# Seven edits to a two-layer trunk: panels asked for before the small vectors, attention's scores group by group, layer 1's first tiles one after the other, and an end that scales its copies

## The reference, cut to what matters

```python
for i in range(DEPTH):
    mod = silu(cond) @ w_ada + b_ada                       # shift, scale, gate, twice
    h = rmsnorm(x, norm_mix) * (1.0 + sc1) + sh1
    mix = mixer_ab(h) if i % 2 == 0 else mixer_c(h)        # layer 0; layer 1
    x = x + g1 * mix
    h = rmsnorm(x, norm_ffn) * (1.0 + sc2) + sh2
    x = x + g2 * ((silu(h @ w_gate) * (h @ w_up)) @ w_down)
return rmsnorm(x, final_norm)
# mixer_ab, attention of a query group: p = softmax(q @ k.T * scale); o = p @ v
# mixer_c, for each of 4 heads: q, k, v, g from h @ w_in; bidirectional scan with
#   decays; y = rmsnorm(y); out += (silu(g) * y) @ w_out
```

## Time and profile before

| | us |
|---|---|
| runs, median (lowest, highest) of 3 | 2038.24 (2036.21, 2041.35) |
| the profiled execution, its own time | 2041.52 |
| its span | 2039.9 |
| PE, weight loads, DVE, ACT busy | 95%, 89%, 58%, 28% |
| mean DMA rate, bytes | 91 GB/s, 185 MB |

### The profile page before, as it was taken

The page is one execution under the profiler, slowest core; times in us unless marked ns, Lnnn a source line. Parts: engine busy times, 40 slices in busy tenths (PEclk is TensorE's granted clock), DMA queues, the critical chain, the costliest instruction groups (busy, mean ns, idle before and its releaser), DMA issues.

```text
span 2039.9 us, 31926 instructions
## 1 busy us (share of the span) xinstructions
PE 1928.6 (95%) x12949; PEld 1821.2 (89%) x12949; DVE 1173.0 (58%) x1836; ACT 564.1 (28%) x721; POOL 45.0 (2%) x80
## 2 busy tenths in 40 slices
PE   6998978989999999989999999999998999999997
PEld 4997656889999999988798798798798999999997
DVE  4977657787847756767465565565566232323235
ACT  1325642132212211224223233232333221221221
POOL 0000010000000000000000000000000000000000
PEclk8999988989999999999999999999998999999998
DMA  8521044225334533332121121122112213222211
GB/s 267 177 65 42 2 145 130 84 62 163 125 104 130 174 109 104 108 99 92 62 92 63 62 92 63 62 73 82 60 44 62 83 62 83 73 71 83 63 62 52
DMA packets 213535, 185.27 MB, mean 91 GB/s; under 512 B 10865, under 2 KB 198705, under 8 KB 213425
## 3 DMA queue, kind: packets, MB, share of 16 engines
q1 hardware_dynamic: 209504, 172.27, 27.5%
q0 software_dynamic: 3616, 11.29, 1.7%
q10 hardware_dynamic: 305, 0.10, 0.0%
HBM read 176.42 MB, written 7.21 MB: 90 GB/s over the span
## 4 chain that ended last, share of the span: by engine, by line
PE 81%; DVE 11%; ACT 3%; issue 2%; DMA 1%; SPq 0%; ACTq 0%; DVEq 0%
PE acc L599 58%; PE acc L1077 4%; PE acc L613 4%; PE acc L1108 2%; PE acc L1124 2%; DVE xT L1689 2%; DVE tbuf L1713 1%; PE mix L1097 1%; PE acc L636 1%; PE mix L682 1%; PE mix L1077 1%; ACT probs L1342 1%; PE mix L816 1%; DVE w_lo L1586 1%; DVE sq_sum L1610 1%
## 5 line engine op out<-in xcount | busy, mean ns | idle before, releaser
L599 PE MATMUL acc<-h_hi,w_hi 128*128 128x320 f32 x2016 | 466.1, 313 | 15.5 <-DVE qk L2217 6.1
L599 PE MATMUL acc<-h_lo,w_hi 128*128 128x320 f32 x2016 | 462.2, 311 | 1.0 <-DVE h_lo L2040 1.0
L599 PE MATMUL acc<-h_hi,w_lo 128*128 128x320 f32 x2016 | 462.2, 311 | 0.0
L1181 ACT ACTIVATE w_hi<-raw 128x2048 fp32r<-128x2048 f32 x112 | 214.3, 1914 | 654.8 <-PE acc L599 649.9
L599 PEld LDWEIGHTS acc<-h_hi,w_hi 128*128 128x128 f32 x2016 | 337.9, 189 | 20.9 <-issue 17.6
L1586 DVE TENSOR_TENSOR w_lo<-raw,w_hi 128x2048 fp32r<-128x2048 f32 x112 | 256.6, 2291 | 167.7 <-ACT w_hi L1181 164.9
L599 PEld LDWEIGHTS acc<-h_lo,w_hi 128*128 128x128 f32 x2016 | 339.5, 189 | 1.8 <-DVE h_lo L2040 1.7
L599 PEld LDWEIGHTS acc<-h_hi,w_lo 128*128 128x128 f32 x2016 | 339.8, 189 | 0.0
L1689 DVE SCALAR_TENSOR_TENSOR xT<-acc,mod,xT 128x128 f32<-128x128 f32 (+2 forms) x288 | 108.8, 433 | 163.2 <-PE acc L599 160.2
L1713 DVE SCALAR_TENSOR_TENSOR tbuf<-ada_raw,scond,tbuf 128x256 f32<-128x256 f32 x392 | 172.7, 482 | 7.0
L2067 DVE TENSOR_TENSOR gu<-silu_g,acc 128x640 f32<-128x640 f32 x44 | 36.1, 821 | 224.6 <-PE acc L599 219.9
(11 more groups left out here) (365 smaller groups left out, 2541.3 us busy)
## 6 DMA issues: line engine op xcount, KB each, us to landing
ada_raw<-in_l_w_ada_dram SPq DMA_DIRECT2D x68, 512.0 KB, 4.8
raw<-in_l_w_in_dram SPq DMA_DIRECT2D x64, 512.0 KB, 4.5
raw<-in_l_w_gate_dram SPq DMA_DIRECT2D x44, 512.0 KB, 4.1
raw<-in_l_w_up_dram SPq DMA_DIRECT2D x44, 512.0 KB, 5.3
raw<-in_l_w_down_dram SPq DMA_DIRECT2D x32, 512.0 KB, 4.5
raw<-in_l_w_out_dram SPq DMA_DIRECT2D x24, 512.0 KB, 4.6
raw<-in_l_w_ada_dram SPq DMA_DIRECT2D x18, 512.0 KB, 4.7
raw<-in_l_w_down_dram SPq DMA_DIRECT2D x16, 384.0 KB, 3.8
```

The costliest lines, as they stand in the source:

```text
L599: last = mm(acc[:, 2 * r + b, 0:HALF], w[:, k * cols + col:k * cols + col + P], x[:, k, b * HALF:(b + 1) * HALF], start=(k == 0 and n == 0 ...
L1181: act(w_hi[s][:, :], raw[s][:, :], ACT.Copy).then_inc(S[f"w_hi{s}"], ac.up(f"w_hi{s}"))
```

## The change

- A. SP no longer waits for `setup_in`. The scale's four jobs (4 to 7) come first. The mods of the first eight go to banks of `acc`. DVE makes scale and gain as soon as its four are there, norms four tiles, makes w_lo, and then the shift.
- B. `ADA_PLACES` moves.
- C. `scores_of` has the group as its outer loop and waits for each group's own exp.
- D. The head's first two tiles come one after the other (`tile_a` with `at` for head 0); V's wait for the banks is split in two.
- E. y's copy is two halves of `acc`, each with PE's wait split, and the prompt's part last.
- F. ACT makes `x_gain` = xT times the final gain, tile by tile, during the last product; PE turns `x_gain` into seven banks; ACT and DVE in turn scale by 1/rms as they copy. ACT loads the root's table earlier. `rms_back` and L2250 go.
- G. The POOL memset of `a_rep` tells on the semaphore `pads`.

```diff
+        FIRST_JOBS = (4, 5, 6, 7, 0, 1, 2, 3)
...
-            eng.wait_ge(S["setup_in"], 12 * 16)
-            for n in range(8):
-                if n == 7:
+            for i, n in enumerate(FIRST_JOBS):
+                if i == 7:
                     panel(w_in[:, :, cols[0]:cols[0] + W])
                 first_panel(n)
...
-            for n in range(8):
-                ada_job(0, n, n > 0, first=True)
-                if n == 5:
+            for i, n in enumerate(FIRST_JOBS):
+                ada_job(0, n, FIRST_JOBS[i - 1] if i else None, first=True)
+                if i == 5:
                     rms_sum()
...
-            ADA_PLACES = [(1, 1), (1, 4), (2, 3), (3, 1)]
+            ADA_PLACES = [(1, 2), (2, 0), (2, 4), (3, 1)]
...
-                if p:
-                    eng.wait_ge(S["exp_done"], 2 + 2 * p)
-                for at, n, from_ in [(0, 512, P), (512, P, N)]:
-                    for g in range(2):
+                for g in range(2):
+                    if p:
+                        eng.wait_ge(S["exp_done"], 2 + 2 * p - 1 + g)
+                    for at, n, from_ in [(0, 512, P), (512, P, N)]:
...
-                first_pair(next_job(), mixed)
-                s = next_job()
-                for c in range(2):
-                    tile_a(s, h_hi, h_lo, KT, c * P)
-                for r in range(2):
-                    eng.wait_ge(S[f"acc_free{r}"], pe.now(f"acc_free{r}"))
+                for j in range(2):
+                    s = next_job()
+                    for c in range(2):
+                        tile_a(s, h_hi, h_lo, KT, c * P, at=mixed if j == c == 0 else None)
                 for j in range(2):
                     s = next_job()
                     for t in range(TT):
+                        if j == 0 and t in (0, 2):
+                            eng.wait_ge(S[f"acc_free{t // 2}"], pe.now(f"acc_free{t // 2}"))
...
                 tile_a(s, h_hi, h_lo, KT, 0)
+                eng.wait_ge(S["yr_read"], pe.next("yr_read"))
                 rms_sum()
...
-            rms()
             for n in range(2 * TT):
+                if n == 3:
+                    rms_sum()
+                    for r in range(2):
+                        eng.wait_ge(S[f"acc_free{r}"], pe.now(f"acc_free{r}"))
                 if t == 0:
-                    eng.wait_ge(S["final_ready"], pe.next("final_ready"))
+                    eng.wait_ge(S["xg_ready"], pe.next("xg_ready", KT // 2))
...
+                            if j == 2:
+                                act(ada_row[:, 0:1], ones[:, 0:1], ACT.Sqrt)
+                            for k in (2 * j, 2 * j + 1):
+                                eng.wait_ge(S["x_final"], ac.next("x_final"))
+                                ins = act(x_gain[:, k, :], xT[:, k, :], ACT.Copy, scale=vec[:, FIN + k:FIN + k + 1])
...
-            def modulate(l, m):
+            def modulate(l, m, shifts=None):
...
-                normed(0)
+                ahead = 4 if shifts else 1
+                for k in range(ahead):
+                    normed(k)
+                if shifts:
+                    shifts()
...
-            rms(D, split_lo)
-            eng.wait_ge(S["ada_turned"], v.next("ada_turned", 8))
-            mods(0, 0, 16)
-            gains(0, 0).then_inc(S["gain_ready"], v.up("gain_ready"))
...
+            def scales():
+
+                mods_of_first(8).then_inc(S["dve"], v.up("dve"))
+                eng.wait_ge(S[v.last], v.ended())
+                gains(0, 0).then_inc(S["dve"], v.up("dve"))
+                eng.wait_ge(S[v.last], v.ended())
+
+            def shifts():
+
+                split_lo()
+                mods_of_first(0).then_inc(S["mod_read"], v.up("mod_read"))
+                eng.wait_ge(S[v.last], v.ended())
+                eng.sem_inc(S["gain_ready"], v.told("gain_ready"))
+
+            rms(D, scales)
+            modulate(0, 0, shifts)
...
-                eng.tensor_copy(yR[:, :, 0:N_CTX], mix[:, 0, :].rearrange("p (a n) -> p a n", a=VT))
-                eng.tensor_copy(yR[:, :, N_CTX:], acc[:, :, :]).then_inc(S["yr_read"], v.up("yr_read"))
+                eng.tensor_copy(yR[:, 0:2, N_CTX:], acc[:, 0:2, :]).then_inc(S["yr_read"], v.up("yr_read"))
+                eng.tensor_copy(yR[:, 2:4, N_CTX:], acc[:, 2:4, :])
+                ins = eng.tensor_copy(yR[:, :, 0:N_CTX], mix[:, 0, :].rearrange("p (a n) -> p a n", a=VT))
+                ins.then_inc(S["yr_read"], v.up("yr_read"))
...
-            rms(D)
-            for k in range(KT):
-                ins = st3(xT[:, k, :], xT[:, k, :], vec[:, FIN + k:FIN + k + 1], rB, ALU.mult, ALU.mult)
+            rms_to_inverse(D)
...
-                    ins = eng.tensor_copy(y_out[:, t, half * 512:(half + 1) * 512], acc[:, n % 4, :])
+                    ins = ts(y_out[:, t, half * 512:(half + 1) * 512], out_bank(n), stt[:, 4, t:t + 1], None, ALU.mult)
```

More of the change, by code:

```diff
@@ L124 @@
 SIGNALS = {
-    "act dve pool": "the engine's last instruction has ended",
+    "act dve": "the engine's last instruction has ended",
     "pool_go": "nothing: GpSimd's place to wait at before a transfer",
@@ L145 @@
     "normed h_hi h_ready": "a tile normed and scaled, its high part, its low part",
-    "x_T x_T_read pads": "x turned, copied; the zeros around the convolved rows",
+    "x_T x_T_read pads": "x turned, copied; the zeros around the convolved rows, then those of the spread log decays",
     "qkv_in xb_in conv_raw conv_ready": "q, k and v off the banks; a tile of x|B|C; two convolved; SiLU of all",
@@ L177 @@
     "state_made fs_ready fs_out0 fs_out1": "a final state made, copied, in DRAM",
-    "yr_read g_in z32_ready yg_hi yg_ready": "y copied; SiLU(g); their product and its parts",
-    "final_ready out_T y_by_act y_by_dve": "half of the features normed; a piece turned, copied by ScalarE, by VectorE",
+    "yr_read g_in z32_ready yg_hi yg_ready": "half of y's features copied; SiLU(g); their product and its parts",
+    "x_final xg_ready out_T y_by_act y_by_dve": "a tile of x final, times its gain; a piece turned; normed by ScalarE, by VectorE",
     "out": "a result is in DRAM",
@@ L348, in trunk_kernel @@
         sb.at = ret_end
+        sb.at = h_at
+        x_gain = sb("x_gain", [P, KT, N])
         sb.at = phase_at
@@ L597, in tile_a @@
                             eng.wait_ge(S[came], pe.next(came))
+                        if at and n != 1:
+                            name = ("h_hi", "h_ready")[n // 2]
+                            eng.wait_ge(S[name], at[name] + k + 1)
                         for b in range(2):
@@ L643, in ada_turn @@
                 for c in range(2):
-                    last = mm(ADA[:, l, bass.ds(n * 2 + c, 1), :].rearrange("p o c -> p (o c)"),
-                              ada_row[:, c * P:(c + 1) * P], fold[:, :], start=True, stop=True)
+                    first = l == 0 and n < 8
+                    out = first_mods(8 * (n >= 4))[:, n % 4 * 2 + c, :] if first else ADA[:, l, n * 2 + c, :]
+                    last = mm(out, ada_row[:, c * P:(c + 1) * P], fold[:, :], start=True, stop=True)
                 last.then_inc(S["ada_turned"], pe.up("ada_turned"))
@@ L893, in _ @@
             jobs = iter(ADA_PE)
-            ada_next = lambda: (lambda n: ada_job(0, n, n > ADA_PE[0]))(next(jobs))
+            ada_next = lambda: (lambda n: ada_job(0, n, n - 1 if n > ADA_PE[0] else None))(next(jobs))
             ada_next()
@@ L1567, in _ @@
             root()
+            ac.skip("rinv", 9)
+            eng.wait_ge(S["rinv"], ac.next("rinv"))
             for n in range(2 * TT):
@@ L1571, in _ @@
                     eng.wait_ge(S["out_T"], n + 1)
-                    ins = act(y_out[:, t, half * 512:(half + 1) * 512], acc[:, n % 4, :], ACT.Copy)
+                    ins = act(y_out[:, t, half * 512:(half + 1) * 512], out_bank(n), ACT.Copy, scale=stt[:, 4, t:t + 1])
                     ins.then_inc(S["y_by_act"], ac.up("y_by_act"))
@@ L1661, in modulate @@
                         normed(k + 1)
-                    eng.wait_ge(S["normed"], v.made["normed"] - (k + 1 < KT))
+                    if ahead == 4 and 1 <= k <= KT - 4:
+                        eng.wait_ge(S["h_ready"], v.made["h_ready"])
+                        normed(k + 3)
+                    eng.wait_ge(S["normed"], v.made["normed"] - min(KT - 1 - k, max(ahead - 1, 1)))
                     eng.wait_ge(S["h_hi"], v.next("h_hi"))
```

55 lines of the change are left out of this document (32 added, 23 removed).

## The result

The changed kernel runs in 2015.11 us (median of 4, 2014.17 to 2017.46) against 2039.8 (4 runs beside it, 2036.21 to 2042.0): ratio 0.9882, 95% interval 0.9864 to 0.9901. The forecast was 2016.5. The profiled execution took 2014.17 with a span of 2012.6, that is 27.3 us less than the span before.

The account below looks back on a forecast made before the run. TensorE (PE), busy 95% of the span, was taken as the bound, so only its waits or low-clock stretches could shrink. −4.0 − 3.7 + 7 − 14 − 7.0 = −21.7 from 2038.2 gave 2016.5 us, range 2003 to 2026.

Parts of the forecast that it names:

- A, −4.0: Start: panels requested right behind x bring layer 0's first product from 50.40 to near 46.1; −4.0 us, between −5.2 and −1.5.
- which no panel moves: Start: DVE's squares bind next, ending at 32.88 + 0.82 = 33.70, whenever the panels land.
- B, −3.7: First input projections: asking for the modulation's sum later removes PE's idle and the clock dip behind it; −3.7 us, between 0 and −3.8.
- so the 2.10 us of idle go: First input projections: DVE's product is ready before PE reaches place (1,2) near 70.5, ending PE's 2.10 us wait.
- ready near 67.6: First input projections: DVE's first modulation product, taking 7.28 us, is ready near 67.6, before its place near 70.5.
- the next wait takes its place: First input projections: the bound of 0 gain, where a wait at (2,0) replaces the one removed.
- C, +7: Attention: the new score order loses the two groups' overlap, +0.60 us for some 13 pairs; +7, bounds −2.3 and +13.6.
- rival 1: Attention: the scores still overlap, giving −2.3 us instead of +7 and 2007 in all; chance .27.
- D and E, −14: Layer 1's head loop: 17.4 us of PE's waits go, against 0.6 kept and 3.1 lost in head 0; −14, bounds −10, −15.
- 5.1 go: Head loop: each head's first tile needs only the bank freed a tile earlier, so 5.1 us of PE's waits go.
- F, −7.0: End: early table load and turned pieces bring the first scaled copy from 2030.46 to near 2023.55; −7.0 us, between −5.5 and −7.8.
- Rivals 2 to 5: Low clock in head 0 2019 (.08); attention at low clock 2083 (.06); small vectors starve 2042 (.04); new waits 2038 (.02).

## Why the prediction held, point by point

The time came out within 1.4 us, and part of that is luck. C was wrong in sign, by 8.3 us in the two profiles, and B's mechanism failed. Of C's 8.3 us, 2.7 were taken back by terms that came out smaller and by what was not foreseen. Another 2.6 are in the profiles and not in the medians (27.3 us gained there, 24.7 here), and 1.6 went because the kernel before stood at 2039.8 beside the changed one and not at 2038.2. A second set of runs gave 2018.3 against 2039.2, 20.9 us.

- *A, −4.0.* 3.39 in the two profiles. With the start's scatter the first product is at 49.2 in the mean of nine profiles with A (45.3 to 53.3) and at 50.4 and 52.0 in two without: 2 us, not clear of the scatter. My bounds, −5.2 and −1.5, spoke of transfers, while most of the scatter is the clock's. DVE's squares, "which no panel moves", ended at 32.55, 1.15 earlier than I took, since x was turned earlier; from there the steps came within 1.1 us of the forecast (way back done at 39.6, four tiles at 43.5, the low part at 45.7, first product at 47.0). The sum of squares starts at 31.7 to 37.6 with A and at 36.0 and 37.6 without. Missing was what norming ahead does behind the first product.
- *B, −3.7.* 3.24 in the profile, but the step from the place (1,2) to "so the 2.10 us of idle go" failed: alone it gave +0.6 (65.13 against 64.51). The time came from A, which takes three tiles' norming (2.75 us) out of DVE's way and so has the product ready 5.8 us earlier, at 69.0. My "ready near 67.6" follows from no row: before it was ready at 74.8, and A's 4.0 would make that 70.8; "the next wait takes its place" was my bound of 0, and it is what happens without A.
- *C, +7.* The step that failed: "If matmuls start in the order in which they stand, the second group's 512 can't start before the first's 128". It can, and rival 1 came true in this part: −2.1 by the kernel with C undone, at the same clock, and −1.3 in the two profiles. The price of a lost overlap was too low as well (1.30 a pair, not 0.85). The rule of the Trainium skill ("TensorE: Matmul & The Clock Gate", Part 3: Packing small matmuls) that matmuls start and end in the order of the program does not hold for the starts of products on different rows of the array here (203.63 before 204.28); that they run concurrently does (1.36 us for both groups, 1.34 for one).
- *D and E, −14.* −13.7 (from 9.22 to 22.94), with two errors in it. Head 0 costs +3.08 by the kernel with the pair back (+3.1 foreseen; +1.98 in the two profiles, where v's wait went too). y and v went as reckoned, and at the third tile all 2.5 and not 1.9. "5.1 go" at the head's first tile failed: 3.8 of it stayed as idle time for which the profile shows no releaser, where the loop turns. In its place came one dip of the clock fewer (1.54) and some 0.6 a head more than the idle time that went (v to v fell by 3.93 between heads 1 and 2, where the idle time fell by 3.35), whose cause is not shown.
- *F, −7.0.* −7.05, and 7.0 by the kernel with the old end.
- *Not foreseen:* 2.0 us lost in the norm after the heads, where PE's clock was 0.5 in the sums after (0.51 from 1517 to 1522) and 0.73 before; the thirteen profiles other than the kernel before have 5.4 to 6.0 us there and only that one 3.9. Gained: 1.5 between the scan's sum of squares (362.3 after, 370.0 before) and that of layer 0's second norm, which comes and goes between equal kernels with the clock: nine profiles have 45.3 us there, each with 3.4 us or more at half clock, and five have 43.8 with none. Before, it was low from 372.6 for 3.4 us.

```profile
1517.00:1522.00 5.00, 4.23 (x20) 4.23 (x20) 0.66 (x1) 1.33 (x2) 0.00 (x0) 0.51 0.00 0
```

With C at −2.1 the sum would have been −30.8, which is 3.5 more than the profiles gained and 6.1 more than the medians did: the wrong sign of C hid that the other terms together were too large. Rivals 2 to 5 did not come: the low clock in head 0 ended near 913 after, setup's vectors did not starve (PE turned x from 11.5 on, and from 11.5 to 13.1 in the nine profiles with this start, against 12.4 before). What stays open is when the clock falls at the start: the first product of one start differs by 8 us with it, and I changed nothing that moved it for sure.

## What to carry to other kernels

A wait that goes with two edits at once has to be tried in all four corners: the place was moved for it, and the time came from DVE's work done before PE needed anything. Where a producer paces two consumers' tiles, let the second run a few steps behind the first: it needs its banks later and still leaves little work behind the last step. A wait at the top of a loop may cover idle time that is there anyway, so read it as an upper bound of what its removal gives. And compare stages between profiles, and only at the same clock: C looked worth 0.5 us between two profiles of which one had 3.4 us more at half clock, and is worth 2.1. Most of the spread of the spans lay in two stretches, the first 50 us (8.1 us between profiles of one start) and the one from attention's last scores to the scan's sum of squares, where no edit was made: 114.7 to 121.3 us, with 3.4 to 24 us at half clock.

## What the runs showed of the hardware that I had not expected

- Matmuls on the upper and lower 64 rows of the array pass each other: a product of the second group starts before an earlier one of the first (four records of 512 columns and none of 128 in 203.30 to 204.25), and two groups' products take 1.36 us together, 1.34 and 1.31 each alone.
- Behind the sums of squares in a head (20 matmuls of one column) PE ran at half clock for some 3 us in some heads and not in others, at 1.54 us each, in 1 to 4 of 4 heads. Two versions that kept only some of the waits had it more often than the kernel before, which had them all; what decides is open.
- Where the loop over the heads turns, PE stands idle for 1.0 to 1.5 us with no releaser in the profile, in all twelve profiles in which the first tile waits for one pair of banks; with the wait for both pairs (1.70) it doesn't show. That the turn itself is the cause was not tested.
- How long the clock stays at half (3.4 or 6.8 us at the start of the attention) is worth 1.1 to 1.7 us there with C's waits and 0.9 with the old ones.
